# Hybrid trunk step with routed experts: how the last gate of the expert stage is raised, who issues the y rows, and where the last gate product runs

## What is computed

```python
h2 = modulate(x, norm_g[i, 1], sh2, sc2)
x = x + g2[:, None, :] * moe(h2, router_w, router_b, moe_w_gate[i], moe_w_up[i], moe_w_down[i])
...
y = rmsnorm(x, final_g)
```

```python
hid = jax.nn.silu(hg) * hu * gates[..., None].astype(t.dtype)
out = jnp.einsum('tef,efd->td', hid, w_down)
```

## Time and profile before

| | us |
|---|---|
| median of 3 executions | 1120.44 |
| lowest and highest | 1118.19, 1123.35 |
| the profiled execution | 1122.56 |
| its span, first to last instruction | 1120.8 |
| PE busy in it | 874.0 (78%) |
| DVE busy | 322.8 (29%) |
| ACT busy | 205.7 (18%) |
| POOL busy | 77.0 (7%) |

### The profile page before, as it was taken

One profiled execution on the slowest core, in us unless ns is written; L12 is line 12 of the kernel. 1 busy time (PEld: TensorE's weight loads), 2 busy tenths in 40 slices (PEclk: granted clock), 3 DMA queues, 4 the chain that ended last, 5 costly groups with the idle time before them and its releaser, 6 DMA issues.

```text
span 1120.8 us, 13474 instructions
## 1 busy us (share of the span) xinstructions
PE 874.0 (78%) x5430; PEld 445.3 (40%) x5430; DVE 322.8 (29%) x683; ACT 205.7 (18%) x371; POOL 77.0 (7%) x144
## 2 busy tenths in 40 slices
PE   2657564799999999435999997957399999999820
PEld 0323232344333333124888776844244433333200
DVE  2594535011011101074340038246300111010109
ACT  1230420100010001032110192235110100010014
POOL 1000000100011000000000000000000110011014
PEclk9777676899999999956999998978589999999975
DMA  8994789999899999499000000002999999999973
GB/s 274 414 415 161 285 358 361 395 421 372 300 364 418 421 421 421 175 334 341 1 1 1 1 1 0 1 6 104 395 421 420 341 311 395 421 421 420 422 263 112
DMA packets 58832, 311.27 MB, mean 278 GB/s; under 512 B 8173, under 2 KB 11549, under 8 KB 28041
## 3 DMA queue, kind: packets, MB, share of 16 engines
q1 hardware_dynamic: 43088, 272.42, 61.0%
q10 hardware_dynamic: 9345, 20.14, 5.1%
q0 software_dynamic: 6336, 17.83, 4.2%
HBM read 294.68 MB, written 21.28 MB: 282 GB/s over the span
## 4 chain that ended last, share of the span: by engine, by line
PE 40%; DVE 6%; DMA 4%; ACT 2%; POOLq 1%; SPq 1%; issue 1%; ACTq 0%; POOL 0%; PEldq 0%; PEld 0%; DVEq 0%
PE bank L628 12%; PE bank L823 11%; PE bank L650 6%; PE bank L857 3%; PE bank L865 3%; PE bank L840 3%; DMA ring<-in_moe_w_down_dram 3%; POOLq L354 1%; DVE work L1160 1%; PE bank L597 1%; DVE work L1357 1%; SPq L410 1%; ACT hT L942 1%; DVE hT L1160 1%; DVE work L1347 1%
## 5 line engine op out<-in xcount | busy, mean ns | idle before, releaser
L628 PE MATMUL bank<-ring,work 128*32 128x512 f32 (+1 forms) x1280 | 240.3, 593 | 2.8 <-DMA hT<-in_moe_w_up_dram 2.8
L650 PE MATMUL bank<-ring,work 128*32 128x512 f32 (+1 forms) x992 | 155.6, 593 | 4.3 <-DMA ring<-in_moe_w_down_dram 4.3
L823 PE MATMUL bank<-hT,ring 128*128 128x272 f32 x512 | 120.5, 398 | 10.8 <-ACTq L354 10.0
L628 PEld LDWEIGHTS bank<-ring,work 128*32 128x32 f32 (+1 forms) x1280 | 72.3, 118 | 116.0 <-issue 113.6
L628 PE MATMUL bank<-work 128*32 128x512 f32 (+1 forms) x592 | 113.6, 594 | 3.0 <-DMA work<-in_moe_w_up_dram 3.0
L823 PEld LDWEIGHTS bank<-hT,ring 128*128 128x128 f32 x512 | 98.4, 193 | 33.2 <-ACTq L354 10.8
L628 PE MATMUL bank<-hT,work 128*32 128x512 f32 (+1 forms) x368 | 90.4, 607 | 1.7 <-DVE work L1483 1.7
L650 PEld LDWEIGHTS bank<-ring,work 128*32 128x32 f32 (+1 forms) x992 | 50.8, 118 | 94.0 <-issue 92.1
L1500 DVE COPY work<-bank 128x512 f32<-128x512 f32 x22 | 15.2, 691 | 218.6 <-PE bank L650 218.6
L530 PE MATMUL bank<-ring,work 128*32 128x512 f32 x384 | 52.3, 690 | 15.7 <-DMA ring<-in_w_mod_dram 15.7
L1492 DVE TENSOR_TENSOR work<-work,bank 128x512 f32<-128x512 f32 x22 | 15.1, 688 | 146.2 <-PE bank L628 146.2
(11 more groups left out here) (242 smaller groups left out, 908.7 us busy)
## 6 DMA issues: line engine op xcount, KB each, us to landing
ring<-in_moe_w_down_dram SPq DMA_DIRECT2D x58, 1024.0 KB, 14.9
ring<-in_w_mod_dram SPq DMA_DIRECT2D x48, 1024.0 KB, 16.4
ring<-in_moe_w_up_dram SPq DMA_DIRECT2D x40, 1024.0 KB, 12.3
ring<-in_moe_w_gate_dram SPq DMA_DIRECT2D x36, 1024.0 KB, 13.3
work<-in_moe_w_up_dram SPq DMA_DIRECT2D x18, 1024.0 KB, 21.4
hT<-in_moe_w_gate_dram SPq DMA_DIRECT2D x14, 1024.0 KB, 8.1
work<-in_moe_w_gate_dram SPq DMA_DIRECT2D x14, 1024.0 KB, 14.6
work<-y_rows ACTq DMA_DIRECT2D x16, 512.0 KB, 7.2
```

Of the source, the lines that this page charges most:

```text
L628: last = pe.matmul(bank[part][c0:c0 + cn, :], xe[b][:, k, c0:c0 + cn], w[:, kk, :], start=(k == 0), stop=(k == DC - 1))
L650: last = pe.matmul(bank[2 + half][c0:c0 + cn, :], hidT[b][:, k, c0:c0 + cn], w[:, kk, half * HALF:(half + 1) * HALF], start=(k == 0), stop ...
L823: last = pe.matmul(bank[2 * (i % 2) + h][:, 0:H2], w[:, k, :], hT[:, k, h * H2:(h + 1) * H2], start=(k == 0), stop=(k == DC - 1))
```

## The change

Four edits. First, POOL reads the number of extra rounds and branches ahead of its wait for the scatters, and raises the gate by a plain semaphore increment, without a drain; the waits for the scatters stand behind the branch (and once more inside it, for the case with extra rounds). Second, the y rows of the second experts (k = 1) are issued by SP, in a new function `load_second`, which waits for the gate; ACT issues the five loads with k = 0. Third, in `last_rows` the gate product moves from POOL to DVE, between the sum and the residual of the same group. Fourth, the loops of `last_rows` on ACT and DVE are one step apart where they were two: ACT squares group j - 1 behind the scaling of group j, and DVE norms group j - 1 behind the residual of group j.

```diff
+            def load_second(l):
+
+                sp.wait_ge(gate_sem, 4 * (6 + 6 * l))
+                for j in range(NT):
+                    w = TW[j]
+                    sp.dma_start(yl[j][1][0:w, :], y_rows[l][T + j * P:T + j * P + w, :]).then_inc(y_loaded[j], 16)
...
             load_overflow(0)
+            load_second(0)
             load_lru(0)
...
             sp.dma_start(final_row, final_g.partition_broadcast(P)).then_inc(last_loaded, 16)
+            load_second(1)
...
-                for j in range(NT + 2):
+                for j in range(NT + 1):
...
-                    if j >= 2:
-                        i, w = j - 2, TW[j - 2]
+                    if j >= 1:
+                        i, w = j - 1, TW[j - 1]
                         act.wait_ge(last_x, i + 1)
...
-                    for k in range(2):
-                        act.dma_start(yl[j][k][0:w, :], y_rows[l][k * T + j * P:k * T + j * P + w, :]
-                                      ).then_inc(y_loaded[j], 16)
+                    act.dma_start(yl[j][0][0:w, :], y_rows[l][j * P:j * P + w, :]).then_inc(y_loaded[j], 16)
...
+                        dve.wait_ge(r["y_summed"], j + 1)
+                        dve.tensor_tensor(y, y, gate_last[j][0:w, :], ALU.mult).then_inc(last_gated, 1)
+                        dve.wait_ge(last_gated, j + 1)
+                        dve.tensor_tensor(y, y, x_last[j][0:w, :], ALU.add).then_inc(last_x, 1)
...
-                for b in range(2):
-                    pool.wait_ge(q[f"scattered{b}"], 16 * (l + 1) * OF_PARITY[b])
                 o = ov[l]
                 n_ov = pool.value_load(ovinfo[0:1, NOV:NOV + 1], min_val=0, max_val=NOV)
                 with pool.If(n_ov > 0):
+                    for b in range(2):
+                        pool.wait_ge(q[f"scattered{b}"], 16 * (l + 1) * OF_PARITY[b])
...
-                stage_end(pool, "pool")
+                for b in range(2):
+                    pool.wait_ge(q[f"scattered{b}"], 16 * (l + 1) * OF_PARITY[b])
+                passed["pool"] += 1
+                pool.sem_inc(gate_sem, 1)
+                pool.wait_ge(gate_sem, 4 * passed["pool"])
...
-                pool.wait_ge(last_loaded, 16 * 5)
-                for j in range(NT):
-                    w = TW[j]
-                    pool.wait_ge(r["y_summed"], j + 1)
-                    pool.tensor_tensor(yl[j][0][0:w, :], yl[j][0][0:w, :], gate_last[j][0:w, :], ALU.mult
-                                       ).then_inc(last_gated, 1)
```

More of the change, by code:

```diff
@@ L1341, in last_rows @@
             def last_rows(r):
-                for j in range(NT + 2):
+                dve.wait_ge(last_loaded, 16 * 5)
+                for j in range(NT + 1):
                     if j < NT:
                         w = TW[j]
+                        y = yl[j][0][0:w, :]
                         dve.wait_ge(r["y_scaled"], j + 1)
-                        dve.scalar_tensor_tensor(yl[j][0][0:w, :], yl[j][1][0:w, :], wts[0:w, 1, j:j + 1],
-                                                 yl[j][0][0:w, :], ALU.mult, ALU.add).then_inc(r["y_summed"], 1)
-                    if 1 <= j < NT + 1:
+                        dve.scalar_tensor_tensor(y, yl[j][1][0:w, :], wts[0:w, 1, j:j + 1], y, ALU.mult, ALU.add
+                                                 ).then_inc(r["y_summed"], 1)
+                        dve.wait_ge(r["y_summed"], j + 1)
+                        dve.tensor_tensor(y, y, gate_last[j][0:w, :], ALU.mult).then_inc(last_gated, 1)
+                        dve.wait_ge(last_gated, j + 1)
+                        dve.tensor_tensor(y, y, x_last[j][0:w, :], ALU.add).then_inc(last_x, 1)
+                    if j >= 1:
                         i, w = j - 1, TW[j - 1]
-                        dve.wait_ge(last_gated, i + 1)
-                        dve.tensor_tensor(yl[i][0][0:w, :], yl[i][0][0:w, :], x_last[i][0:w, :], ALU.add).then_inc(last_x, 1)
-                    if j >= 2:
-                        i, w = j - 2, TW[j - 2]
                         dve.wait_ge(last_std, i + 1)
```

## The result

| | before | changed |
|---|---|---|
| median, us (6 executions each) | 1121.55 | 1111.87 |
| lowest to highest, us | 1118.19 to 1124.02 | 1111.22 to 1113.64 |
| span of the profiled execution, us | 1120.8 | 1110.1 |
| POOL busy in it, us | 77.0 | 61.5 |
| DVE busy in it, us | 322.8 | 320.3 |

The ratio of the times is 0.9917, with a 95% interval from 0.9898 to 0.9935: 9.3 us less, and the interval reaches from 7 to 11. The forecast was 1111.1 in a range from 1106.5 to 1116.5, and faster by more than 0.5% had the most weight; the whole interval lies beyond 0.5%. The median of the kernel before is that of six executions here, 1.1 above the one of three that the forecast started from.

What follows compares the result with a forecast made beforehand. PE's matmuls and weight loads set the whole time; the changed stretches are bound by POOL's gate, then ACT's issuing and DVE. Terms 2.6 + 2.4 + 0.8 + 3.5 = 9.3 took 1120.44 to 1111.1 us, range 1106.5 to 1116.5.

Steps and rivals of the forecast that it cites:

- What bounds the kernel: At both gates all engines stand in one chain behind POOL; from 1089.35 in layer 1 DVE is the bound.
- the forecast 5.0: POOL's read, branch and drain leave the path at both gates: 2.6 us gained in layer 0, 2.4 in layer 1.
- Rival 1: POOL is held 1.7 us behind a scatter whatever comes next: 1114.5, or 1116.1 if the read is held; chance 0.15.
- The issuers: Behind layer 1's gate, five fewer ACT issues let scaling begin at 4.8 instead of 5.57 us: 0.8 gained.
- Layer 0's 0: Splitting the loads gains nothing in layer 0, where DVE waits for the second group's scaling, 8.0 us behind the gate.
- The product: In `last_rows`, the gate product on DVE cuts first sum to end from 29.10 to 25.56 us: 3.5 gained.
- Uneven queues: Loads behind the gates: second halves come late, up to 3 us in each layer; time 1116, chance 0.12.
- The gate did wait for POOL and for nobody else: Judges a rival at the gates: the changed gate would wait for someone else; next to no chance.
- The LRU did not run longer at the low clock: Judges a rival: LRU matmuls stay longer at 1.2 GHz, 1140.7 us with 128 more of them; chance 0.03.
- ACT kept up: In `last_rows`, ACT's third scaling, now behind the first square, has about 1 us to spare: no cost.
- The clock gave back nothing: At the LRU's start, 1.3 us comes back if PE's clock rises at the same time, nothing if with the work.
- The sum: Whole kernel: 2.6 and 2.4 at the gates, 0.8 for issuing, 3.5 in `last_rows`, together 9.3 us.

Runs made afterwards that it cites:

- the gate alone: Kernel before with only POOL's gate changed: number read and branched on ahead of the scatter wait, plain increment for the drain; ratio 0.9959, 4.6 us less.
- the late drain: Changed kernel with layer 0's later POOL drain put off until DVE has summed the first group; ran once, 1116.67 us.

## Why the prediction was right

**What bounds the kernel** held at the gates. The gate is opened by POOL, its 2.5 and 2.7 us are the read, the branch and the drain, and 2.43 and 2.61 of them were gained. With the gate alone 2.4 of the 2.6 reached the LRU, and behind the gate of layer 1 every step was as long as before; the time, 4.6 us less in an interval from 2 to 7, agrees with the forecast 5.0. Rival 1 held that the 1.7 was POOL's and not the drain's. It falls by the 0.09 in the chain, and the late drain shows that the cost comes with the instruction, whenever it is put. Why it is 1.69 stays open. My reason for taking the full gain, that a second drain has 0.05, was right in its result and thin as an argument: a drain at another time has its 1.69 too.

**The issuers** are the term that was mis-sized. The sum had 0.8 for layer 1 and the runs 0.2. The step that failed is "scaling waits for its landing, 4.8 behind the gate". I took the landing from the kernel before, where the first group's two loads are first in one queue. On two queues the group's halves come in side by side, with the second group's loads issued 0.4 behind them, and the later half landed 5.3 behind the gate, the other at 4.5. The kernel with one queue on SP starts scaling at 5.0. That it is the second group's loads that hold the first group's is argued from these landings; no run kept them back. The sentence ahead of it, that ACT's own issuing held the first group, was right for ACT but a second limit stood close behind. (The spacing of the first four landings in the kernel before was misread too: it is 1.4 to 2.0 us, not 1.1 to 2.0. Nothing in the sum hangs on it.) Layer 0's 0 held: 8.27 in the changed kernel, in a spread of 7.9 to 8.5 over kernels with one queue and with two. The Trainium skill, "DMA: Bandwidth & Descriptors", section "Issuing engines are not separate DMA queues", has it that the transfers interleave and only sequencer time is saved; the traces agree, with 0.2 us of the saved 2.6 us of issue time arriving.

**The product** held: 3.3 for 3.5. The missing 0.2 come from steps that are a hair longer: 5.11 per group for 5.05. Start to start, the second group's sum, gate product, and residual with reciprocal take 1.31, 1.26 and 1.34, where the sum had 1.30, 1.24 and 1.31. One reading was too simple: DVE was not without a rest from 1089.35 on. Behind its first sum it was idle for 1.39, waiting for ACT's second scaling, and two of its sums were held by POOL. The term did not suffer, since it set the new order against the whole 29.10. The wait inside DVE's instructions is gone with POOL's. The rule of the Trainium skill, "SBUF — State Buffer", section "Who interferes with whom", named that wait, and the trace after agrees: 1.28 for 3.18 in the norm and 1.28 for 3.37 in the sum, with no POOL instruction beside them.

**The other rivals.** Uneven queues would have put layer 0's second group at 10 or more behind the gate; it is at 8.27. The gate did wait for POOL and for nobody else. The LRU did not run longer at the low clock, as the rows below show.

**What was left at nothing** stayed there. ACT kept up, though the third group's scaling moved behind the first root (it ends at 1089.54, DVE wants it at 1090.74). The loads for `last_loaded` were in. The clock gave back nothing that can be told: the LRU's first 128 matmuls took 31.50, against 31.77, and over the fourteen traces of the study 31.04 to 32.65, in no order with their start. The granted clock is at 1.00 from 518 on, some 4 us behind the first matmul as before, though the LRU starts 4.2 earlier. So the rise moved with the work and did not stay at its time; in the other traces it came 3 to 6 us behind the first matmul:

```profile
513.67 31.50 PE bank L832 x128
...
513.00:518.00 5.00, 4.33 (x11) 3.32 (x12) 0.42 (x3) 0.60 (x1) 0.00 (x0) 0.54 1.06 384
518.00:523.00 5.00, 5.00 (x23) 4.16 (x22) 0.00 (x0) 0.00 (x0) 0.00 (x0) 1.00 1.05 387
```

**The sum** was 9.3, the stretches have 8.5, and the times 9.3 with 7 to 11. That the middle value agrees so well with the sum is luck: in the traces the issuers' term fell short by 0.6 and the product by 0.2, and single executions of one program spread over 5 us and more.

## What to carry to other kernels

At a barrier, look at what the last engine does between the event that everybody waits for and its increment: here a register read, a branch and a drain of 1.7 us, of which the first two could stand earlier and the drain was not needed on this path. Do not split a group's loads over two queues because the issue is slow without asking when the group's last half lands. And where an instruction is more than twice as long in one place as in another, look for the engine beside it before counting its own work.

## What was not expected of the hardware

A drain on POOL behind an indirect transfer costs 1.69 us even 8 us after the landing, with POOL idle, and a second one 0.05. Put directly behind the issue, it lasted until 0.8 behind the scatter's landing, and until 0.1 to 0.2 behind a gather's.

Two 512 KB loads that are first in two queues, with four more behind each, landed 4.5 and 5.3 us from their issue; first and second in one queue, with the second issued 0.36 later, 3.5 and 4.6.

A scatter of 128 rows landed in 2.7 us once the 512 KB loads ahead of it that read one 4 KB row 128 times were gone, against 4.4 to 5.1 with them. Whether it is the reading of one row or only the added megabyte that makes their tail was not tried.
